# The end of a two-layer backbone kernel: overflow count read early, first gathered rows combined under the last expert, row sums as accumulated output, squares on ScalarE

## The reference

```python
def _moe(h, w_router, b_router, w_gate, w_up, w_down):
    scores = softmax(h @ w_router)                     # 16 experts in 4 groups
    # best group by its top-2 sum, then the top 2 experts in it
    combine = ...                                      # weight of each expert for each token, 2 non-zero
    act = silu(h @ w_gate) * (h @ w_up) * combine      # d_ff = 512
    return act @ w_down

x = _layer_norm(ALPHA * x + g1 * y, ln1_g, ln1_b)
f = _moe(x * (1 + sc2) + sh2, ...)
x = _layer_norm(ALPHA * x + g2 * f, ln2_g, ln2_b)      # eps 1e-5, mean and variance over 1024 channels
```

## Time and profile before

| | |
|---|---|
| time, median of 3 runs | 816.76 us (815.81 to 817.58) |
| profiled execution | 815.22 us, span 813.5 us |
| busy, share of the span | PE 88%, DVE 71%, PEld 69%, ACT 53%, POOL 7% |
| chain that ended last, by engine | PE 74%, DVE 11%, ACT 6%, DMA 5%, issue 3% |
| its costliest lines | PE L1128 70%, DMA of w_ada 3%, DMA of constants 2%, PE L1516 2% |
| DMA `out<-arena`, 512 KB | 2.6 us from issue to landing |
| mean granted TensorE clock | 0.94 |

### The profile page before, as it was taken

One profiled execution on the slowest core, in us unless ns is written; L12 is line 12 of the kernel. 1 busy time (PEld: TensorE's weight loads), 2 busy tenths in 40 slices (PEclk: granted clock), 3 DMA queues, 4 the chain that ended last, 5 costly groups with the idle time before them and its releaser, 6 DMA issues.

```text
span 813.5 us, 12342 instructions
## 1 busy us (share of the span) xinstructions
PE 712.0 (88%) x4722; PEld 559.4 (69%) x4722; DVE 578.6 (71%) x834; ACT 432.1 (53%) x596; POOL 57.8 (7%) x90
## 2 busy tenths in 40 slices
PE   2699989899898989999399598999999999999870
PEld 0487978788586978874155486887888888887730
DVE  2559676687685355754554796999999989999765
ACT  1546854254123345660021466888888888888510
POOL 3040000000002000014000020000000000000400
PEclk9699989999999999999779699999999999999995
DMA  9995499899544741239400899999999999998421
GB/s 333 337 326 197 164 341 365 281 395 400 200 173 121 271 165 54 104 37 266 172 0 1 332 411 395 388 396 398 397 398 398 401 401 399 399 397 321 156 80 52
DMA packets 91506, 220.05 MB, mean 271 GB/s; under 512 B 3335, under 2 KB 3631, under 8 KB 91455
## 3 DMA queue, kind: packets, MB, share of 16 engines
q1 hardware_dynamic: 84512, 197.66, 65.4%
q0 software_dynamic: 6528, 21.56, 8.6%
q10 hardware_dynamic: 415, 0.14, 0.1%
HBM read 179.99 MB, written 39.36 MB: 270 GB/s over the span
## 4 chain that ended last, share of the span: by engine, by line
PE 74%; DVE 11%; ACT 6%; DMA 5%; issue 3%; POOL 1%; SPq 0%; DVEq 0%; ACTq 0%; POOLq 0%
PE ps L1128 70%; DMA ring<-in_w_ada 3%; DMA iota<-in_consts 2%; PE ps L1516 2%; ACT w_hi L803 1%; PE ps L1535 1%; DVE arena L1696 1%; DMA arena<-in_b_in 1%; DVE w_lo L1678 0%; ACT arena L913 0%; DVE arena L1827 0%; DVE small L1955 0%; DVE arena L1826 0%; DVE arena L1959 0%; DVE arena L1960 0%
## 5 line engine op out<-in xcount | busy, mean ns | idle before, releaser
L2123 DVE TENSOR_TENSOR w_lo<-arena,w_hi 128x1024 fp32r<-128x1024 f32 x96 | 114.8, 1221 | 15.4 <-ACT w_hi L1027 14.0
L2123 DVE TENSOR_TENSOR w_lo<-ring,w_hi 128x1024 fp32r<-128x1024 f32 x96 | 114.9, 1221 | 8.5 <-ACT w_hi L1027 6.9
L1027 ACT ACTIVATE w_hi<-ring 128x1024 fp32r<-128x1024 f32 x96 | 101.0, 1064 | 17.3 <-PE ps L1128 14.5
L1027 ACT ACTIVATE w_hi<-arena 128x1024 fp32r<-128x1024 f32 x96 | 101.1, 1066 | 15.3 <-PE ps L1128 15.2
L1128 PE MATMUL ps<-h_hi,w_lo 128*128 128x384 f32 x288 | 102.8, 357 | 5.6 <-DVE w_lo L1678 4.4
L1128 PE MATMUL ps<-w_hi,slot_tokens_lo 128*128 128x512 f32 x256 | 103.1, 403 | 4.0 <-DVE w_lo L2123 4.0
L1128 PE MATMUL ps<-w_hi,slot_tokens_hi 128*128 128x512 f32 x256 | 100.8, 394 | 0.0
L1128 PE MATMUL ps<-w_lo,slot_tokens_hi 128*128 128x512 f32 x256 | 100.5, 393 | 0.0
L1128 PE MATMUL ps<-h_hi,w_hi 128*128 128x384 f32 x288 | 98.0, 340 | 0.0
L1128 PE MATMUL ps<-h_lo,w_hi 128*128 128x384 f32 x288 | 97.9, 340 | 0.0
L1678 DVE TENSOR_TENSOR w_lo<-ring,w_hi 128x1024 fp32r<-128x1024 f32 x44 | 53.7, 1225 | 32.9 <-ACT w_hi L803 32.0
(11 more groups left out here) (352 smaller groups left out, 1123.8 us busy)
## 6 DMA issues: line engine op xcount, KB each, us to landing
slot_rows<-arena SPq DMA_DIRECT2D x12, 2048.0 KB, 17.2
ring<-in_w_in SPq DMA_DIRECT2D x11, 2048.0 KB, 12.4
ring<-in_w_ada SPq DMA_DIRECT2D x10, 2048.0 KB, 10.0
ring<-in_w_gate SPq DMA_DIRECT2D x8, 2048.0 KB, 15.1
ring<-in_w_up SPq DMA_DIRECT2D x8, 2048.0 KB, 14.7
ring<-in_w_down SPq DMA_DIRECT2D x8, 2048.0 KB, 11.6
arena<-in_w_gate SPq DMA_DIRECT2D x8, 2048.0 KB
arena<-in_w_down SPq DMA_DIRECT2D x8, 2048.0 KB, 11.3
```

The source lines that it names most:

```text
L1027: act.activation(w_hi[:, at_ % 4, :], raw[:, q * QUARTER:(q + 1) * QUARTER], ACT.Copy).then_inc(S["hi_ready"], 1)
L2123: tt(w_lo[:, at_ % 4, :], raw[:, q * QUARTER:(q + 1) * QUARTER], w_hi[:, at_ % 4, :].bitcast(F32), ALU.subtract).then_inc(S["lo_dve"], 1)
```

## The change

On ScalarE, TensorE and VectorE the register load of the overflow count moves from behind the first expert pass into it: on VectorE and ScalarE right behind `last_rows` in expert 0, on TensorE in the last expert between the transposes and the down projection. The branch stays behind the pass. ScalarE scales the gathered rows of tile 0 ahead of the copy of the last expert's results (in the case without overflow), and VectorE combines them ahead of its first wait for TensorE. TensorE waits for the halves of the last results one by one. In the second norm the BATCH_NORM_STATS are gone: the mean comes from an accumulated output of the operation that adds the residual, the variance from an accumulated Square on ScalarE with the negated mean as bias, followed by the root. VectorE's order is mix 0, mix 1, result 0, mix 2, result 1, result 2. A root of a constant stands ahead of ScalarE's loop. SyncE and GpSimd are unchanged.

```diff
@@ ScalarE, expert_pass and behind it
                 if base == 0:
                     last_rows()
+                    act.wait_ge(S["route_ready"], 2)
+                    over = act.value_load(over_i[0:1, 0:1], min_val=0, max_val=T)
...
-                out_rows_sb(n, pair, 1, True)
-            expert_pass(0)
-            act.wait_ge(S["route_ready"], 2)
-            over = act.value_load(over_i[0:1, 0:1], min_val=0, max_val=T)
+                if base:
+                    out_rows_sb(n, pair, 1, True)
+                return over
+            def first_picked():
+                act.wait_ge(picked[0], 32)
+                act.activation(PICK[:, 0, 0, :], PICK[:, 0, 0, :], ACT.Identity, scale=pick_e[:, 0, 0:1]).then_inc(S["picked_scaled"], 1)
+            over = expert_pass(0)
             with act.If(over > P):
+                out_rows_sb(NE - 1, NPAIR - 1, 1, True)
                 expert_pass(NE)
                 expert_pass(2 * NE)
-            act.wait_ge(picked[0], 32)
-            act.activation(PICK[:, 0, 0, :], ...)
+                first_picked()
+            with act.Else():
+                first_picked()
+                out_rows_sb(NE - 1, NPAIR - 1, 1, True)
+            act.activation(rstd, eps, ACT.Sqrt)
             for i in range(NT):
                 act.wait_ge(S["ln_var"], NT + i + 1)
-                act.activation(rstd, mv_stats[:, 13:14], ACT.Sqrt, bias=eps).then_inc(S["ln_std"], 1)
+                act.activation(PICK[:, 1, i, :], X1[:, i, :], ACT.Square, bias=row_mean[:, i:i + 1], accum_out=row_sq[:, i:i + 1]).then_inc(S["ln_std"], 1)
+                act.wait_ge(S["ln_std"], NT + 2 * i + 1)
+                act.activation(row_rstd[:, i:i + 1], row_sq[:, i:i + 1], ACT.Sqrt, bias=eps, scale=1.0 / D).then_inc(S["ln_std"], 1)
@@ TensorE
                 act_transpose(n)
+                over = None
+                if base == 0:
+                    pe.wait_ge(S["route_ready"], 2)
+                    over = pe.value_load(over_i[0:1, 0:1], min_val=0, max_val=T)
                 down(n, True)
...
-            pe.wait_ge(S["out_sb"], 2 * NE)
             for i in range(NT):
                 for half, bank in enumerate(MIX_BANKS[i]):
+                    if i == 0:
+                        pe.wait_ge(S["out_sb"], 2 * NE - 1 + half)
@@ VectorE
                 if base == 0:
                     last_rows()
+                    over = dve.value_load(over_i[0:1, 0:1], min_val=0, max_val=T)
                 with dve.Fori(0, NPAIR - 1) as i:
...
             dve.wait_ge(S["g2_in"], 16 * 2)
+            dve.wait_ge(S["picked_scaled"], 1)
+            first = PICK[:, 0, 0, :]
+            step(stt(first, PICK[:, 1, 0, :], pick_e[:, 1, 0:1], first, ALU.mult, ALU.add))
+            step(tt(first, first, g2_b[:, 0, :], ALU.mult))
+            step(tt(X1[:, 0, :], X1[:, 0, :], first, ALU.add))
+            def mixed_rows(i):
+                y = PICK[:, 0, i, :]
                 for half, bank in enumerate(MIX_BANKS[i]):
                     cols = slice(half * G, (half + 1) * G)
                     dve.wait_ge(S["mixed"], 2 * i + half + 1)
-                    step(tt(y[:, cols], ps[:, bank, :], g2_b[:, s, cols], ALU.mult))
-                step(tt(X1[:, i, :], X1[:, i, :], y, ALU.add))
-                norm(i, 2, NT + i, "out_tile")
+                    step(tt(y[:, cols], ps[:, bank, :], g2_b[:, min(i, 1), cols], ALU.mult))
+                step(stt(X1[:, i, :], X1[:, i, :], 1.0, y, ALU.mult, ALU.add, accum_out=row_mean[:, i:i + 1]))
+                step(ts(row_mean[:, i:i + 1], row_mean[:, i:i + 1], -1.0 / D, None, ALU.mult), "ln_var")
+            def result(i):
+                x = X1[:, i, :]
+                dve.wait_ge(S["ln_std"], NT + 2 * i + 2)
+                step(stt(x, x, row_mean[:, i:i + 1], ln_b[:, 2, :], ALU.add, ALU.mult))
+                step(dve.reciprocal(row_rstd[:, i:i + 1], row_rstd[:, i:i + 1]))
+                step(stt(x, x, row_rstd[:, i:i + 1], ln_b[:, 3, :], ALU.mult, ALU.add), "out_tile")
+            mixed_rows(0)
+            mixed_rows(1)
+            result(0)
+            mixed_rows(2)
+            result(1)
+            result(2)
```

More of the change, by code:

```diff
@@ L466, in build @@
         last_w = kept[:, 43:46]
+        row_mean = kept[:, 46:49]
+        row_sq = kept[:, 49:52]
+        row_rstd = kept[:, 52:55]
         pick_diag = moe(6800, 512).rearrange("p (c i t) -> p c i t", c=2, i=2)
@@ L1108, in expert_pass @@
                 hi(n, 11, down, 3)
-                out_rows_sb(n, pair, 1, True)
-            expert_pass(0)
-            act.wait_ge(S["route_ready"], 2)
-            over = act.value_load(over_i[0:1, 0:1], min_val=0, max_val=T)
+                if base:
[5 more added lines that the diff above has]
+            over = expert_pass(0)
             with act.If(over > P):
+                out_rows_sb(NE - 1, NPAIR - 1, 1, True)
                 expert_pass(NE)
                 expert_pass(2 * NE)
-            act.wait_ge(picked[0], 32)
-            act.activation(PICK[:, 0, 0, :], PICK[:, 0, 0, :], ACT.Identity, scale=pick_e[:, 0, 0:1]).then_inc(S["picked_scaled"], 1)
+                first_picked()
[3 more added lines that the diff above has]
+            act.activation(rstd, eps, ACT.Sqrt)
             for i in range(NT):
                 act.wait_ge(S["ln_var"], NT + i + 1)
-                act.activation(rstd, mv_stats[:, 13:14], ACT.Sqrt, bias=eps).then_inc(S["ln_std"], 1)
+                act.activation(PICK[:, 1, i, :], X1[:, i, :], ACT.Square, bias=row_mean[:, i:i + 1], accum_out=row_sq[:, i:i + 1]).then_inc(S["ln_std"], 1)
+                act.wait_ge(S["ln_std"], NT + 2 * i + 1)
+                act.activation(row_rstd[:, i:i + 1], row_sq[:, i:i + 1], ACT.Sqrt, bias=eps, scale=1.0 / D).then_inc(S["ln_std"], 1)
         @block.tensor
@@ L1590, in expert_pass @@
                 act_transpose(n)
+                over = None
+                if base == 0:
+                    pe.wait_ge(S["route_ready"], 2)
+                    over = pe.value_load(over_i[0:1, 0:1], min_val=0, max_val=T)
                 down(n, True)
-            expert_pass(0)
-            pe.wait_ge(S["route_ready"], 2)
-            over = pe.value_load(over_i[0:1, 0:1], min_val=0, max_val=T)
+                return over
+            over = expert_pass(0)
             with pe.If(over > P):
@@ L1949, in _ @@
             step(stt(chunk(YM, H - 1), ps[:, 2, 0:T], colsA[:, A_MLG + H - 1:A_MLG + H], chunk(MO, H - 1), ALU.mult, ALU.mult), "ym_done")
[L1951 to L1960, removed]
             def with_cols(dst, src, cols):
@@ L2181, in expert_pass @@
                     lo(n, 8 + q, down, q)
-            expert_pass(0)
-            over = dve.value_load(over_i[0:1, 0:1], min_val=0, max_val=T)
+                return over
+            over = expert_pass(0)
             with dve.If(over > P):
@@ L2190, in _ @@
             dve.wait_ge(S["g2_in"], 16 * 2)
-            for i in range(NT):
-                s = min(i, 1)
-                y = PICK[:, 0, i, :]
[L2194 to L2197, removed]
-                    step(tt(X1[:, i, :], X1[:, i, :], y, ALU.add))
+            dve.wait_ge(S["picked_scaled"], 1)
[4 more added lines that the diff above has]
+            def mixed_rows(i):
+                y = PICK[:, 0, i, :]
                 for half, bank in enumerate(MIX_BANKS[i]):
```

## The result

The changed kernel takes 806.52 us (median of 4 runs, 805.01 to 807.43) against 816.28 of the kernel before: ratio 0.9878, 95% interval 0.9856 to 0.9901. The profiled execution took 805.01, its span 803.3. Measured a second time, beside new runs of before, it took 808.37 (6 runs, 806.59 to 810.21), ratio 0.9907 (0.9880 to 0.9934). So 7.6 to 10.0 us are won (a ratio of 0.9907 is 7.6 of 816.3) where 4.7 were forecast; both medians lie under the range that I gave, the second one barely.

A forecast was written before the change was run, and what follows sets the result against it. TensorE was taken to bound the experts, VectorE's chain the end: 5.6 us won there, less 0.9 for VectorE's load, gives 4.7, so 816.76 - 4.7 = 812.1 us, range 808.4 to 814.5.

The forecast's parts named there:

- TensorE's start: First mixing product after the last expert: stays at 777.91, 3.06 us after the last down product; earlier load wins 0.
- My own sign of being wrong: At the mixing's start: forecast wrong if TensorE's first mixing product starts under 2 us after the last expert's last product.
- First gathered rows: Tile 0, under the last expert: ScalarE scales near 772, VectorE done before 777; all 3.84 us leave the path.
- My other bound: TensorE's mixing start with the first half's copy at 775.4, 2.5 us earlier; as rival "branch shorter" 809.6 us, chance 0.12.
- Waiting for one half: TensorE's mixing start: waiting for one half of the last rows wins nothing, both halves being there at 775.98, before 777.8.
- clock not lowered: Rival, tile 0's mixing products: at 2.4 GHz they take 0.86 instead of 1.7 us each; 1.7 sooner, 810.4; chance 0.18.
- Both rivals together: Mixing start and clock: TensorE's branch up to 2.5 us shorter with the high clock as well, 807.9; no joint chance given.
- Loads: Register loads at new places: VectorE's in expert 0 costs 0.9 us (bounds 0 and 0.9), TensorE's 0, ScalarE's 0, at most 0.9.
- Row statistics: Second norm: 2.10 us per tile go; ScalarE's square and root, 1.75 us, stay hidden; one table load.
- the term of the accumulated output: VectorE's residual sum in the second norm: 1.28 us plus 0.2 for accumulating, at most another pass of 1.42.
- The new chain: VectorE's mixing and results end at 800.8 instead of 806.4, 5.6 us won, with waits for TensorE of 0.9, 0.1 and 1.9.

The follow-up runs named there:

- experiment 1: Changed kernel with TensorE's register load put back between the last down projection and the branch: 810.43 us, ratio 0.9923.
- experiment 8: The changed kernel itself, unaltered, measured again and traced a second time (the second trace): 808.37 us, ratio 0.9907.
- experiment 7: Changed kernel with a second register load of the same count, value unused, directly ahead of TensorE's branch: 810.22 us, ratio 0.9926.
- experiment 3: Kernel before with only TensorE's register load moved ahead of the last down projection: 815.68 us, ratio 0.9993.
- before with and without filling products: Kernel before with seven extra 128x128 products around the last expert's transposes: 814.83 us, ratio 0.9976; and the kernel before itself, 816.28 us.
- experiment 10: Changed kernel with VectorE's load late and two gathered products of tile 1 first: 804.54 us with seven extra products around the last transposes, 805.95 without.
- experiment 9: Changed kernel without TensorE's register load, branch and overflow passes: 807.74 us, ratio 0.9896.

## Why the prediction was wrong

The step that failed is "TensorE's start": "the earlier load gives TensorE nothing". The gap before the mixing shrank by 2.27 us and the products ran at 2.4 GHz for another 1.67: 3.9 of the 4.6 us by which the second trace beats the forecast (9.3 won against 4.7). Putting the load back takes 3.5 of them away (experiment 1). My own sign of being wrong, a first mixing product under 2 us after the last down product, came true.

- *First gathered rows.* Right: ScalarE at 771.20 (forecast near 772), VectorE from 772.95 to 776.76 (before 777), the copy not delayed.
- *TensorE's start.* I kept 777.91, 3.06 us after the last down product; measured 1.68 and 0.79. I had read the branch's 5.98 us as a fetch that waits until the queue is empty, because its packet came behind the last matmul's start. That fell: in experiment 8 the packet is there ahead of the last down product. In all thirteen traces with a branch it ends 2.4 to 2.9 us after that packet starts, and the packet starts 1.3 to 2.0 us after the branch where the load is far from it, 2.5 to 3.5 where one is next to it. So the load, which looked free beside queued matmuls, cost twice: 0.7 to 0.9 us of a later branch and a longer branch, by 1.1 us in experiments 1 and 7 and 2.2 in experiment 3. My other bound, 2.5 us earlier, held the truth (2.3); I gave it 0.12. Waiting for one half, which I had put at nothing, also counts now, by at least 0.33 us: in experiment 8 the products start at 780.32, the second half is there at 780.65.
- The rule of the Trainium skill on the fetch of a taken branch (Runtime: NRT & Kernel Launch, Instruction fetch mechanics) agrees with the traces: every one with the branch shows the packet, the one without it doesn't. What failed is what I drew from it, that nothing could be won by reading the count early. The stall can begin under queued work: in experiment 8 the branch starts 3.74 us ahead of the end of the down products and only 0.62 us of it is left behind them.
- *Clock.* The rival "clock not lowered" came with the shorter gap: 12.25 us of mixing instead of 13.92 in all eight traces with a gap of 1.87 or less. Behind gaps of 2.72 to 4.27 it was 13.92 to 13.95 each time, at 1.96 once so and once so. I had treated the two rivals as separate chances; in twelve of fourteen traces gap and clock go together, and only at 1.96 they don't decide each other. Both rivals together stood at 807.9 in my working, below the range that I then gave.
- *Loads.* Right: 0.96 on VectorE (0.9), nothing on ScalarE (from the first diagonal to the first weights 1.16 us, 1.17 before), nothing on TensorE (its wait ahead of the down products is 1.41 us in both).
- *Row statistics.* Mechanism right, the term of the accumulated output too large: 1.27 us for sum and accumulator where I took 1.52, 0.5 us over two tiles. Squares and roots were hidden, and no second table load came.
- *The new chain.* Right in its form: VectorE waits 1.88 us for tile 1's second half (forecast 1.9), 0.35 for its first (forecast 0.1), nothing for tile 2. For tile 0 it doesn't wait in the first trace and 0.27 and 0.17 us in the second, where I had 0.9 by the low clock. From TensorE's first mixing product to the end it is 20.8 us; I had 22.9, the 1.67 of the clock and 0.5 of the accumulation apart.
- The first trace had a down projection of 5.79 us besides, which is luck and was mostly given back by the gap.

Sum against the second trace, which shares the lowered clock of before in the down projection: load +0.96 (of which 0.85 shows at the start of the down products), down -0.21, gap -2.27, from there to the end -7.68 (28.46 to 20.78): 9.3 us less in the trace. The forecast for these was +0.9, 0, 0 and -5.6. Of the -7.68, 1.67 are the clock and 0.5 the accumulated output.

## What to carry to other kernels

Move a register load that a branch needs away from the branch. On TensorE the branch could then run beside queued products (3.74 of its 4.36 us in experiment 8), and a load next to it cost more than its own length (1.8 us for a load and its register operations of 0.7 in experiment 7). Judge a move like this by the engine that will be late next, not by the one that is late now: alone in the kernel before it was worth nothing, in the traces of the changed one 3.5 us. When one engine's chain is shortened until another's shows, price the clock of that other engine together with its idle gap, since both can change at once.

## What the runs showed of the hardware that I had not expected

- TensorE's taken branch over the two skipped passes lasts 3.77 to 4.49 us with the load far from it (seven traces) and 4.87 to 5.98 with a load next to it (six traces). Why the load delays the fetch stays open. Experiments 1, 3 and 7 each move or add the load alone, but each also shifts the code around the branch by that one load, and no run tells the two apart.
- A faster stretch ahead of a branch hides less of it: the 1.57 us won in the down projection by keeping the clock at 2.4 GHz were followed by a gap longer by 0.9 to 1.5 us (the two traces of the changed kernel, before with and without filling products, the two of experiment 10). Without the branch the gap stays at 0.78 (experiment 9).
- On VectorE reading the accumulator takes 0.08 us, on ScalarE 0.19; both begin about 0.1 us before the operation's own end (779.38 against 779.45, 780.74 against 780.84).
